# A chunked scan: Gram products with the two heads alternating on the array's row halves, and chunk decays read from the running sums by ScalarE

## The chip, the cores and the metric

The kernel runs as one program on one core of one Trainium2 chip. The metric is the device time of one execution in microseconds (us). The engines named below are TensorE (PE, with its weight loads listed as PEld), VectorE (DVE), ScalarE (ACT), GpSimdE (POOL) and the DMA queues that SyncE (SP) issues. They run side by side and wait for each other through semaphores.

## What is computed

Two transformer blocks follow each other on 256 tokens of width 2048, all in float32. The first is a differential attention with a short convolution and a gated feed-forward. The second puts 16 meta tokens ahead (272 tokens in all), and has two branches: a gated linear recurrence (RWKV-7) with 16 heads of 64, and an attention with forget gates. The change lies in the recurrence:

```
def step(S, inp):                       # per head, S is 64 x 64
    r_t, w_t, k_t, v_t, a_t, b_t = inp
    sa = einsum('bhvk,bhk->bhv', S, a_t)
    S  = S * w_t[:, :, None, :] + sa[..., None] * b_t[:, :, None, :] + v_t[..., None] * k_t[:, :, None, :]
    return S, einsum('bhvk,bhk->bhv', S, r_t)
```

`w_t` is a decay per channel. The kernel does not step through 272 tokens. It cuts them into three chunks (16, 128 and 128 tokens) and works with products of whole chunks.

## The kernel before, in words

**The big products.** Nearly all of the time goes into dense layers whose weights come from memory in units of 1 MB (`w_raw`). ACT rounds a unit to `w_hi`, DVE subtracts to get `w_lo`, and PE makes three products (`hi*hi`, `lo*hi`, `hi*lo`) for each tile of 128 x 128 weights.

**The recurrence** runs in eight steps `j`, each for two heads, which lie on partitions 0 to 63 and 64 to 127 of one tile. `rwkv_pe`, `rwkv_act` and `rwkv_dve` hold the instruction streams of a step, written out by hand. The order on an engine is the order of the code. One counting semaphore per engine (`rp`, `ra`, `rd`) carries the names of the steps: `did(("gram", j))` adds one, and `after(("gram", j))` waits for it.

Between the pieces of a step stands `side(n)`. It puts in `n` slots of a dense layer that runs beside the recurrence (lines L468, L470, L472 on PE: six matmuls a slot; L450 on ACT and L455 on DVE prepare its weights). So while PE waits in the recurrence it has other work, as much as is put there. The side work goes on after the recurrence; a slot that isn't used is not lost.

The places in one step that matter here, in order on PE:

- **sums** (L1627 to L1629): for each chunk, the log decays `ld` (stationary) times a table of ones and zeros. L1627 gives the inclusive running sums in PSUM bank 4, L1628 the exclusive ones in bank 3. Both are counted from the chunk's middle: `mid` is 1 for the first half of the chunk, and is subtracted. L1629 gives three more columns for each chunk in bank 5: the sum over the first half, over the second half, and over all.
- ACT then takes exponentials (L1854 to L1857). The last one, over 9 columns, is `eaux`: the decays from a chunk's start to its middle, from the middle to its end, and over all of it.
- DVE builds the scaled tensors `bh`, `kh` and `ar` from them (L1971 to L1975), PE transposes some (**toks**, L1641 and L1645).
- **gram** (L1659, L1661, L1664): the products of `bh` and `kh` with `ar` within each chunk, for each head. A product contracts over the 64 channels of one head, so its operands lie on one half of the partitions. Of each 128 x 128 result, L1659 makes the upper 64 rows and L1661 the lower right quarter (the other quarter is above the diagonal and masked). L1664 makes the 16 x 16 results of the meta tokens. Head `h`, source `n` and chunk `c` go to PSUM bank `2 * n + h`. The 16 x 16 results of both heads lie in bank 4.
- After `gram`, PE does four slots of side work. DVE masks the results and starts to invert a triangular matrix with PE and ACT in turns (L1989, L2026 to L2061; L1675 on PE).
- Later in the step the recurrent `state` is carried from chunk to chunk (L2082 to L2103) with the columns of `eaux`.

One float32 matmul of the code shows as two MATMUL records in the trace, each with its weight load. An f32 product in the dense layers (`fp32r`) shows as one.

Of the kernel before, what the change touches and what calls it, by code (L numbers as in the profile page):

```python
# [48 lines left out]
def constants():  # L49

    p = np.arange(P)
    parts = {}
    parts["ident"] = np.eye(P)
    half = (p[:, None] // RHD) == (p[None, :] // RHD)
    parts["head_sum"] = half.astype(float)
    parts["head_center"] = np.eye(P) - half / RHD
    s, t = p[:, None], p[None, :]
    parts["gram_mask"] = np.concatenate([s < t, s <= t], axis=1)
    parts["upper8"] = (s < t) & (s // 8 == t // 8)
    parts["lower8"] = (s > t) & (s // 8 == t // 8)  # L60
    for m in (16, 32, 64, 128):
        parts[f"join{m}"] = (s // m == t // m) & (s % m < m // 2) & (t % m >= m // 2)

    def sums(n):
        s, t = np.arange(n)[:, None], np.arange(n)[None, :]
        mid = (s <= n // 2 - 1).astype(float)
        incl, excl = (s <= t) - mid, (s < t) - mid
        aux = np.concatenate([mid, 1 - mid, np.ones((n, 1))], axis=1)
        m = np.concatenate([incl, excl, aux], axis=1) * DECAY_SCALE
        return np.concatenate([m, np.zeros((P - n, m.shape[1]))], axis=0)  # L70

    parts["sums"] = sums(P)
    parts["sums_meta"] = sums(META)
    k = np.arange(TOK)[None, :]
    parts["fox_mask"] = np.where(k <= P + META + p[:, None], 0.0, MASKED)
    sel = np.zeros((P, 46))
    sel[:64, 14], sel[64:, 15] = 1, 1
    parts["half_to_row"] = sel
    sel = np.zeros((P, 15))
    sel[:, 7] = 1  # L80
    parts["tile_to_row"] = sel
    parts["causal_tokens"] = s <= t

    dist = 255 - np.arange(SEQ + P - 1)
    n = np.maximum(dist, 0)
    exact = BUCKETS // 2
    nf = np.maximum(n, exact).astype(np.float32)
    large = exact + (np.log(nf / np.float32(exact)) / np.float32(math.log(MAX_DIST / exact))
                     * np.float32(BUCKETS - exact)).astype(np.int32)
    bucket = np.where(n < exact, n, np.minimum(large, BUCKETS - 1))  # L90
    hot = np.zeros((P, dist.size))
    hot[bucket, np.arange(dist.size)] = 1
    parts["bucket_hot"] = hot
    parts["line_mask"] = np.tile(np.where(dist >= 0, 0.0, MASKED), (P, 1))
    at, out = {}, []
    n = 0
    for name, a in parts.items():
        at[name] = (n, n + a.shape[1])
        out.append(a.astype(np.float32))
        n += a.shape[1]  # L100
    return np.concatenate(out, axis=1), at
# [33 lines left out]
def transformer_pair_kernel(nc, a, out, table_at):  # L135

    ctx = ExitStack()
    with ctx:
# [1291 lines left out]
        def place(*shape):  # L1430
            nonlocal at0
            v = area(at0, *shape)
            at0 += int(np.prod(shape))
            return v
# [20 lines left out]

        xs, us = (diff[:, 1, n * P:(n + 1) * P].rearrange("p (h v) -> p h v", h=2) for n in range(2))
        ys = shift[:, 0:SEQ]
        eaux = place(9)
        assert at0 <= ARENA, at0
        y_sq = gm.rearrange("p q (a t) -> p (q a) t", a=2)  # L1460
        rows_kk = small2[0:LANES, 0]
# [124 lines left out]
        def rwkv_pe(side):  # L1586
# [33 lines left out]
            for j in range(8):  # L1620
                side(3)
                pe.wait_ge(*rd.after(("ld", j)))
                for n, t in enumerate(PIECES):
                    rows = t.stop - t.start
                    tb = T["sums_meta" if n == 0 else "sums"]
                    lhs = ld[0:rows, n, :]
                    pe.matmul(psum[:, 4, t], lhs, tb[0:rows, 0:rows], start=True, stop=True)  # L1627
                    pe.matmul(psum[:, 3, t], lhs, tb[0:rows, rows:2 * rows], start=True, stop=True)  # L1628
                    mm = pe.matmul(psum[:, 5, 3 * n:3 * n + 3], lhs, tb[0:rows, 2 * rows:2 * rows + 3],  # L1629
                                   start=True, stop=True)  # L1630
                mm.then_inc(*rp.did(("sums", j)))
                side(2)
                pe.wait_ge(*rd.after(("rk", j)))
# [15 lines left out]

                pe.wait_ge(*rd.after(("bv", j)))  # L1650
                pe.wait_ge(*ra.after(("toks", j)))
                for h in range(2):
                    r = slice(h * RHD, (h + 1) * RHD)
                    for c in range(2):
                        t0 = META + c * P
                        for n, src in enumerate((bh, kh)):
                            o = psum[:, 2 * n + h, 2 * P * c:2 * P * (c + 1)].rearrange(
                                "p (a t) -> p a t", a=2)
                            pe.matmul(o[0:64], src[r, t0:t0 + 64], ar[r, :, t0:t0 + P],  # L1659
                                      start=True, stop=True)  # L1660
                            pe.matmul(o[64:P, :, 64:P], src[r, t0 + 64:t0 + P],  # L1661
                                      ar[r, :, t0 + 64:t0 + P], start=True, stop=True)
                    for n, src in enumerate((bh, kh)):
                        mm = pe.matmul(psum[mh[h], 4, n * META:(n + 1) * META], src[r, 0:META],  # L1664
                                       ar[r, 0, 0:META], start=True, stop=True)
                mm.then_inc(*rp.did(("gram", j)))
# [145 lines left out]
        def rwkv_act(side):  # L1812
# [30 lines left out]
            for j in range(8):  # L1843
# [10 lines left out]
                s.activation(ar[:, 0], psum[:, 3, 0:TOK], ACT.Exp)  # L1854
                s.activation(ar[:, 1], psum[:, 4, 0:TOK], ACT.Exp)
                s.activation(einv, psum[:, 4, 0:TOK], ACT.Exp, scale=-1.0)
                s.activation(eaux, psum[:, 5, 0:9], ACT.Exp).then_inc(*ra.did(("exp", j)))  # L1857
                side(4)
                s.wait_ge(*PEA("toks"))
                s.activation(toks.rearrange("p a b -> p (a b)"), psum[:, 1, :], ACT.Copy)  # L1860
# [51 lines left out]
        def rwkv_dve(side):  # L1912
# [32 lines left out]
            for j in range(8):  # L1945
# [120 lines left out]
                for h in heads:  # L2066
# [12 lines left out]
                    .then_inc(*D_("u0"))  # L2079
                side(1)  # L2080
                v.wait_ge(*PEA("s0"))
                v.tensor_scalar(state, psum[:, 2, 0:RHD], eaux[:, 1:2], None, ALU.mult) \  # L2082
                    .then_inc(*D_("s0"))
                v.wait_ge(*A_("s0"))
                v.tensor_scalar(state_h, state, eaux[:, 3:4], None, ALU.mult).then_inc(*D_("sh1"))
                side(2)
                for c in (1, 2):
                    v.wait_ge(*PEA(f"x{c}"))
                    v.tensor_copy(xs, psum[:, 0:2, 0:RHD]).then_inc(*D_(f"x{c}"))
                    side(1)  # L2090
                    v.wait_ge(*PEA(f"u{c}"))
                    v.tensor_copy(us, psum[:, 3, 0:P].rearrange("p (h v) -> p h v", h=2)) \
                        .then_inc(*D_(f"u{c}"))
                    side(1)
                    if c == 1:
                        v.tensor_scalar(state, state, eaux[:, 5:6], None, ALU.mult).then_inc(*D_("sd"))
                        v.wait_ge(*PEA("y1s1"))
                        v.wait_ge(*A_("sd"))
                        v.scalar_tensor_tensor(out=state, in0=psum[:, 2, 0:RHD], scalar=eaux[:, 4:5],
                                               in1=state, op0=ALU.mult, op1=ALU.add) \  # L2100
                            .then_inc(*D_("s1"))
                        v.wait_ge(*A_("s1"))
                        v.tensor_scalar(state_h, state, eaux[:, 6:7], None, ALU.mult) \  # L2103
                            .then_inc(*D_("sh2"))
                        side(2)
                v.wait_ge(*PEA("y2"))
# [658 lines left out]
```

## Time and profile before

| | |
|---|---|
| median of three runs | 3148.33 us (3145.39 to 3151.86) |
| the profiled execution | 3146.21 us, its span 3144.3 us |
| mean granted clock of TensorE | 0.977 |
| PE busy | 3001.1 us, 95% of the span |
| DVE busy | 1737.0 us, 55% |
| ACT busy | 1238.6 us, 39% |
| L1659, L1661, L1664, L1629 on PE | 128, 128, 64 and 48 records |

A record is one instruction as the profiler saw it. Records of PE overlap, as their ends are modelled; the distance from one start to the next says more of what one costs than its length does. The recurrence lies between about 1500 and 1990 us of the span.

### The profile page before, as it was taken

How to read it: one execution, taken by the hardware profiler on the slowest of the kernel's cores; microseconds unless marked ns; L12 is line 12 of the kernel's file. 1: busy time of each engine (PE TensorE's matmuls, PEld its weight loads, DVE VectorE, ACT ScalarE, POOL GpSimd, SP SyncE). 2: the span in 40 equal slices, each digit the busy share in tenths (PEclk: the TensorE clock that was granted, in tenths of full speed). 3: DMA queues.
4: the chain of work that ended last, by engine and by line, in shares of the span. 5: the costliest groups of instructions: out<-in, count | busy, mean ns of one | idle time of the engine just before them, and what ended most of it. 6: DMA issues, size and time to landing. Idle time of an engine off the chain costs nothing.

```text
span 3144.3 us, 57107 instructions
## 1 busy us (share of the span) xinstructions
PE 3001.1 (95%) x24369; PEld 2880.7 (92%) x24369; DVE 1737.0 (55%) x2618; ACT 1238.6 (39%) x1799; POOL 68.8 (2%) x108
## 2 busy tenths in 40 slices
PE   7999889999999998997999999998999999999999
PEld 6999889999999998997778888796999999999999
DVE  5467556455555446545656566575656454555444
ACT  4345345333334334434323232355334333333343
POOL 1001000000000000000000000000000000000000
PEclk9999899999999998999999999998999999999999
DMA  5665344555555554454222322542554555555553
GB/s 198 205 173 158 114 161 161 185 183 181 185 187 187 186 182 140 160 168 129 79 70 70 83 78 55 147 131 72 188 175 161 187 186 183 182 184 186 187 187 135
DMA packets 370309, 484.89 MB, mean 154 GB/s; under 512 B 12359, under 2 KB 181654, under 8 KB 370150
## 3 DMA queue, kind: packets, MB, share of 16 engines
q1 hardware_dynamic: 362752, 471.55, 47.2%
q0 software_dynamic: 4112, 7.88, 0.9%
q10 hardware_dynamic: 3302, 3.39, 0.3%
q8 instruction: 109, 1.79, 0.2%
q14 instruction: 34, 0.28, 0.0%
HBM read 475.76 MB, written 7.01 MB: 154 GB/s over the span
## 4 chain that ended last, share of the span: by engine, by line
PE 87%; DVE 8%; ACT 3%; issue 1%; DMA 0%; SPq 0%; DVEq 0%; ACTq 0%
PE psum L339 21%; PE psum L337 21%; PE psum L338 21%; PE psum L468 5%; PE psum L472 4%; PE psum L470 4%; PE psum L1675 3%; DVE w_lo L319 1%; PE psum L1659 1%; DVE w_lo L455 1%; ACT w_hi L310 1%; DVE arena L1989 1%; DVE arena L773 0%; PE psum L2391 0%; DVE arena L1992 0%
## 5 line engine op out<-in xcount | busy, mean ns | idle before, releaser
L337 PE MATMUL psum<-act_hi,w_hi 128*128 128x256 f32 (+1 forms) x5840 | 1651.9, 283 | 64.9 <-DVE act_lo L864 18.1
L338 PE MATMUL psum<-act_lo,w_hi 128*128 128x256 f32 (+1 forms) x5840 | 1655.0, 283 | 0.0
L339 PE MATMUL psum<-act_hi,w_lo 128*128 128x256 f32 (+1 forms) x5840 | 1654.1, 283 | 0.0
L319 DVE TENSOR_TENSOR w_lo<-w_raw,w_hi 128x1024 fp32r<-128x1024 f32 x728 | 858.7, 1221 | 894.0 <-ACT w_hi L310 893.9
L310 ACT ACTIVATE w_hi<-w_raw 128x1024 fp32r<-128x1024 f32 x728 | 730.6, 1051 | 1204.7 <-PE psum L339 1204.7
L337 PEld LDWEIGHTS psum<-act_hi,w_hi 128*128 128x128 f32 x5840 | 1111.2, 190 | 72.0 <-issue 32.4
L339 PEld LDWEIGHTS psum<-act_hi,w_lo 128*128 128x128 f32 x5840 | 1112.4, 190 | 0.0
L338 PEld LDWEIGHTS psum<-act_lo,w_hi 128*128 128x128 f32 x5840 | 1104.5, 189 | 0.3
L468 PE MATMUL psum<-act_hi,w_hi 128*128 128x256 f32 (+1 forms) x1280 | 393.5, 307 | 0.9 <-DVE arena L1352 0.9
L472 PE MATMUL psum<-act_hi,w_lo 128*128 128x256 f32 (+1 forms) x1280 | 366.3, 286 | 0.0
L470 PE MATMUL psum<-act_lo,w_hi 128*128 128x256 f32 (+1 forms) x1280 | 366.3, 286 | 0.0
L450 ACT ACTIVATE w_hi<-w_raw 128x512 fp32r<-128x512 f32 x320 | 195.9, 628 | 292.7 <-PE psum L472 278.1
L455 DVE TENSOR_TENSOR w_lo<-w_raw,w_hi 128x512 fp32r<-128x512 f32 x320 | 219.5, 704 | 92.9 <-ACT w_hi L450 92.3
L468 PEld LDWEIGHTS psum<-act_hi,w_hi 128*128 128x128 f32 x1280 | 245.9, 192 | 24.3 <-issue 14.8
L470 PEld LDWEIGHTS psum<-act_lo,w_hi 128*128 128x128 f32 x1280 | 246.2, 192 | 1.0
L472 PEld LDWEIGHTS psum<-act_hi,w_lo 128*128 128x128 f32 x1280 | 246.0, 192 | 0.0
L1675 PE MATMUL psum<-arena 128*128 128x128 f32 (+1 forms) x800 | 125.8, 304 | 23.8 <-DVE arena L2035 17.0
L1675 PEld LDWEIGHTS psum<-arena 128*128 128x128 f32 (+1 forms) x800 | 107.7, 204 | 39.6 <-DVE arena L2035 18.1
L620 DVE TENSOR_TENSOR arena<-psum,rstd 128x256 f32<-128x256 f32 (+1 forms) x200 | 79.3, 420 | 54.8 <-PE psum L339 48.9
L1871 ACT ACTIVATE arena<-psum 128x256 f32<-128x256 f32 x96 | 36.9, 385 | 111.1 <-PE psum L1675 111.1
L1989 DVE TENSOR_TENSOR arena<-psum,tab 64x512 f32<-64x512 f32 (+1 forms) x24 | 20.6, 858 | 31.9 <-PE psum L1664 31.7
L2055 DVE TENSOR_TENSOR arena<-psum,arena 128x256 f32<-128x256 f32 (+1 forms) x56 | 21.3, 393 | 19.7 <-PE psum L1675 17.6
(383 smaller groups left out, 1566.8 us busy)
## 6 DMA issues: line engine op xcount, KB each, us to landing
w_raw<-w_in SPq DMA_DIRECT2D x128, 1024.0 KB, 5.7
w_raw<-w_down SPq DMA_DIRECT2D x88, 1024.0 KB, 5.1
w_raw<-w_gate_up SPq DMA_DIRECT2D x88, 1024.0 KB, 5.0
w_raw<-w_gate SPq DMA_DIRECT2D x44, 1024.0 KB, 5.1
w_raw<-w_up SPq DMA_DIRECT2D x44, 1024.0 KB, 5.1
w_raw<-w_out SPq DMA_DIRECT2D x16, 1024.0 KB, 5.1
w_raw<-w_o SPq DMA_DIRECT2D x16, 1024.0 KB, 5.1
w_raw<-w_branch_a SPq DMA_DIRECT2D x8, 1024.0 KB, 5.0
```

Source lines behind the costliest of these rows:

```text
L310: nc.scalar.activation(w_hi[:, s % 2, 2 * h:2 * h + 2, 0:wd], w_raw[:, s % RAW, 2 * h:2 * h + 2, 0:wd], ACT.Copy).then_inc(hi_ready, 1)
L319: nc.vector.tensor_tensor(w_lo[:, s % 2, 2 * h:2 * h + 2, 0:wd], w_raw[:, s % RAW, 2 * h:2 * h + 2, 0:wd], w_hi[:, s % 2, 2 * h:2 * h + 2, ...
L337: pe.matmul(dst, w1, x1, start=first, stop=False, skip_group_check=True)
L338: pe.matmul(dst, w1, x0, start=False, stop=False, skip_group_check=True)
L339: mm = pe.matmul(dst, w0, x1, start=False, stop=stop and k == UNIT_K - 1, skip_group_check=True)
L450: nc.scalar.activation(side_view(w_hi, u % 2, 4 * n, 4), side_view(w_raw, u % RAW, 4 * n, 4), ACT.Copy).then_inc(hi_ready if n % 2 else si ...
L455: nc.vector.tensor_tensor(side_view(w_lo, u % 2, 4 * n, 4), side_view(w_raw, u % RAW, 4 * n, 4), side_view(w_hi, u % 2, 4 * n, 4).bitcast( ...
L468: pe.matmul(dst, hi[:, k], act_hi[:, k, tok], start=k == 0, stop=False, skip_group_check=True)
L470: pe.matmul(dst, hi[:, k], act_lo[:, k, tok], start=False, stop=False, skip_group_check=True)
L472: mm = pe.matmul(dst, lo[:, k], act_hi[:, k, tok], start=False, stop=k == KT - 1, skip_group_check=True)
L620: nc.vector.tensor_tensor(dst(m), psum[:, m, 0:SEQ], rstd[:, X], ALU.mult) \
L1675: return of_head(h, meta, lambda q, m: pe.matmul(ps(bank, q, m), sl(l, q, m), sl(r_, q, m), start=True, stop=True))
```

## The change

Three edits in the recurrence, and nothing elsewhere.

1. **Gram order.** The outer loop over the heads goes. For each chunk and source, the matmul of head 0 is followed by that of head 1, first for the upper 64 rows, then for the lower quarter. All 16 x 16 products come at the end, with the heads alternating as well. The same matmuls write to the same places.
2. **No third product.** The three columns per chunk (L1629) are no longer computed: 24 matmuls, 48 records in all. ACT reads two columns of each of the running sums: the exclusive sum at a chunk's first token is minus its first half, and the inclusive sum at the last token of a chunk is its second half. So one activation of 9 columns becomes two of 2 columns (`to_mid`, `from_mid`), both from PSUM with a stride.
3. **State.** Where the state was multiplied by the decay over the whole chunk (`eaux[:, 5:6]`), the already scaled `state_h` is multiplied by `from_mid`. That adds a wait for `sh1`, which DVE itself has finished before.

```
-        aux = np.concatenate([mid, 1 - mid, np.ones((n, 1))], axis=1)
-        m = np.concatenate([incl, excl, aux], axis=1) * DECAY_SCALE
+        m = np.concatenate([incl, excl], axis=1) * DECAY_SCALE
...
-                    pe.matmul(psum[:, 3, t], lhs, tb[0:rows, rows:2 * rows], start=True, stop=True)
-                    mm = pe.matmul(psum[:, 5, 3 * n:3 * n + 3], lhs, tb[0:rows, 2 * rows:2 * rows + 3],
-                                   start=True, stop=True)
+                    mm = pe.matmul(psum[:, 3, t], lhs, tb[0:rows, rows:2 * rows], start=True, stop=True)
...
-                for h in range(2):
-                    r = slice(h * RHD, (h + 1) * RHD)
-                    for c in range(2):
-                        t0 = META + c * P
-                        for n, src in enumerate((bh, kh)):
-                            o = psum[:, 2 * n + h, 2 * P * c:2 * P * (c + 1)].rearrange(
-                                "p (a t) -> p a t", a=2)
-                            pe.matmul(o[0:64], src[r, t0:t0 + 64], ar[r, :, t0:t0 + P],
+                for c in range(2):
+                    t0, t1 = META + c * P, META + c * P + 64
+                    for n, src in enumerate((bh, kh)):
+                        o = [psum[:, 2 * n + h, 2 * P * c:2 * P * (c + 1)].rearrange("p (a t) -> p a t", a=2)
+                             for h in range(2)]
+                        for h, r in enumerate(hs):
+                            pe.matmul(o[h][0:64], src[r, t0:t1], ar[r, :, t0:t0 + P], start=True, stop=True)
+                        for h, r in enumerate(hs):
+                            pe.matmul(o[h][64:P, :, 64:P], src[r, t1:t1 + 64], ar[r, :, t1:t1 + 64],
                                       start=True, stop=True)
-                            pe.matmul(o[64:P, :, 64:P], src[r, t0 + 64:t0 + P],
-                                      ar[r, :, t0 + 64:t0 + P], start=True, stop=True)
-                    for n, src in enumerate((bh, kh)):
+                for n, src in enumerate((bh, kh)):
+                    for h, r in enumerate(hs):
                         mm = pe.matmul(psum[mh[h], 4, n * META:(n + 1) * META], src[r, 0:META],
                                        ar[r, 0, 0:META], start=True, stop=True)
...
-                s.activation(eaux, psum[:, 5, 0:9], ACT.Exp).then_inc(*ra.did(("exp", j)))
+                s.activation(to_mid, psum[:, 3, META:META + P + 1:P], ACT.Exp, scale=-1.0)
+                s.activation(from_mid, psum[:, 4, META - 1:META + P:P], ACT.Exp) \
+                    .then_inc(*ra.did(("exp", j)))
...
-                        v.tensor_scalar(state, state, eaux[:, 5:6], None, ALU.mult).then_inc(*D_("sd"))
+                        v.wait_ge(*A_("sh1"))
+                        v.tensor_scalar(state, state_h, from_mid[:, 1:2], None, ALU.mult).then_inc(*D_("sd"))
```

On TensorE, the Gram products of a step before: the end of head 0 and the start of head 1 (64x256 is the upper part, 64x2x64 the lower quarter, 16x16 the meta tokens).

```order
L1659 MATMUL psum<-arena 64x256
L1661 MATMUL psum<-arena 64x2x64
L1659 MATMUL psum<-arena 64x256
L1661 MATMUL psum<-arena 64x2x64
L1664 MATMUL psum<-arena 16x16 x2
L1659 MATMUL psum<-arena 64x256
L1661 MATMUL psum<-arena 64x2x64
```

The same place now, up to the side work behind it (the lines are one or two lower in the changed file).

```order
L1657 MATMUL psum<-arena 64x256 x2
L1659 MATMUL psum<-arena 64x2x64 x2
L1657 MATMUL psum<-arena 64x256 x2
L1659 MATMUL psum<-arena 64x2x64 x2
L1663 MATMUL psum<-arena 16x16 x4
L467 MATMUL psum<-act_hi,w_hi 128x272
```

Each x2 is head 0, then head 1. The 16x16 products stood behind each head, and now stand once behind both.

On ScalarE, the exponentials of a step and what stands behind them, before:

```order
L1854 ACTIVATE arena<-psum 128x272
L1855 ACTIVATE arena<-psum 128x272
L1856 ACTIVATE arena<-psum 128x272
L1857 ACTIVATE arena<-psum 128x9
L450 ACTIVATE w_hi<-w_raw 128x512
L1860 ACTIVATE arena<-psum 128x512
```

And now:

```order
L1853 ACTIVATE arena<-psum 128x272
L1854 ACTIVATE arena<-psum 128x272
L1855 ACTIVATE arena<-psum 128x272
L1858 ACTIVATE arena<-psum 128x2
L1859 ACTIVATE arena<-psum 128x2
L449 ACTIVATE w_hi<-w_raw 128x512
```

One instruction more stands ahead of the rounding of the next side weights.

## Rows read from the trace of the kernel before

**Rows 1.** The page: PE's busy time, and the chain by engine

```profile
PE 3001.1 (95%) x24369; PEld 2880.7 (92%) x24369; DVE 1737.0 (55%) x2618; ACT 1238.6 (39%) x1799; POOL 68.8 (2%) x108
...
PE 87%; DVE 8%; ACT 3%; issue 1%; DMA 0%; SPq 0%; DVEq 0%; ACTq 0%
```

**Rows 2.** Windows, Gram to Gram: us, busy PE, PEld, DVE, ACT, POOL; PEclk, DMA

```profile
1759.28:1819.91 60.63, 57.08 (x461) 49.08 (x460) 37.51 (x98) 17.59 (x44) 2.62 (x5) 0.97 0.27 73
1819.91:1878.57 58.66, 55.05 (x461) 47.55 (x461) 37.47 (x97) 21.85 (x49) 0.00 (x0) 1.00 0.28 72
```

**Rows 3.** Timeline of PE, step 1's Gram products: start, length, [idle before]

```profile
1572.45 0.43 PE L1659 MATMUL psum<-arena 64*64 64x256 f32 x1
1572.46 0.43 PE L1661 MATMUL psum<-arena 64*64 64x128 f32 x2
1572.72 0.38 PE L1659 MATMUL psum<-arena 64*64 64x256 f32 x1
1572.93 0.38 PE L1659 MATMUL psum<-arena 64*64 64x256 f32 x1
...
1574.32 0.26 PE L1664 MATMUL psum<-arena 64*16 64x16 f32 x4
1574.51 0.43 PE L1659 MATMUL psum<-arena 64*64 64x256 f32 x1
...
1576.38 0.26 PE L1664 MATMUL psum<-arena 64*16 64x16 f32 x4
1576.57 0.39 PE L468 MATMUL psum<-act_hi,w_hi 128*128 128x272 f32 x1
```

**Rows 4.** Timeline and line view, L1145: row halves alternate in block one's attention

```profile
184.46 0.93 PE L1145 MATMUL psum<-arena 64*128 64x128 f32 x8
185.31 0.39 PE L468 MATMUL psum<-act_hi,w_hi 128*128 128x256 f32 x1
...
L1145 PE MATMUL psum<-arena x8: 272/374/378, 184.5 to 185.0; 64*128 64x128 f32 x4, 64*128 64x256 f32 x4
```

**Rows 5.** Timeline of PE, running sums of step 1

```profile
1564.37 0.36 PE L1629 MATMUL psum<-tab,arena 16*128 16x3 f32 x2
1564.65 0.49 PE L1627 MATMUL psum<-tab,arena 128*128 128x128 f32 x2
...
1565.34 0.47 PE L1627 MATMUL psum<-tab,arena 128*128 128x128 f32 x2
1565.65 0.39 PE L1628 MATMUL psum<-tab,arena 128*128 128x128 f32 x2
1565.87 0.28 PE L1629 MATMUL psum<-tab,arena 128*128 128x3 f32 x2
1566.01 0.37 PE L468 MATMUL psum<-act_hi,w_hi 128*128 128x272 f32 x1
```

**Rows 6.** Timeline of step 1: from the exponentials to the transposes

```profile
1567.04 0.20 ACT L1857 ACTIVATE arena<-psum 128x9 f32<-128x9 f32 x1
1567.10 1.34 ACT L450 ACTIVATE w_hi<-w_raw 128x512 fp32r<-128x512 f32 x2
...
1567.78 0.69 DVE L455 TENSOR_TENSOR w_lo<-w_raw,w_hi 128x512 fp32r<-128x512 f32 x1 [1.83 <-ACT w_hi L450]
...
1569.22 0.43 DVE L1972 TENSOR_TENSOR arena<-arena 128x272 f32<-128x272 f32 x1
...
1569.71 0.65 PE L1641 MATMUL psum<-tab,arena 128*128 128x128 f32 x4
1570.30 0.51 PE L1645 MATMUL psum<-tab,arena 64*16 64x64 f32 x12
1570.74 0.39 PE L468 MATMUL psum<-act_hi,w_hi 128*128 128x272 f32 x1
```

**Rows 7.** Timeline behind Gram: DVE (step 5), then PE (step 1)

```profile
1824.14 1.22 DVE L1989 TENSOR_TENSOR arena<-psum,tab 64x1024 f32<-64x1024 f32 x1 [3.19 <-PE psum L1664]
...
1584.13 3.53 PE L1675 MATMUL psum<-arena 128*128 128x128 f32 x15 [2.37 <-DVE arena L2035]
```

More of the change, by code:

```diff
@@ L1457, in transformer_pair_kernel @@
         ys = shift[:, 0:SEQ]
-        eaux = place(9)
+        to_mid, from_mid = place(2), place(2)
         assert at0 <= ARENA, at0
@@ L2081, in rwkv_dve @@
                 v.wait_ge(*PEA("s0"))
-                v.tensor_scalar(state, psum[:, 2, 0:RHD], eaux[:, 1:2], None, ALU.mult) \
+                v.tensor_scalar(state, psum[:, 2, 0:RHD], from_mid[:, 0:1], None, ALU.mult) \
                     .then_inc(*D_("s0"))
                 v.wait_ge(*A_("s0"))
-                v.tensor_scalar(state_h, state, eaux[:, 3:4], None, ALU.mult).then_inc(*D_("sh1"))
+                v.tensor_scalar(state_h, state, to_mid[:, 0:1], None, ALU.mult).then_inc(*D_("sh1"))
                 side(2)
@@ L2095, in rwkv_dve @@
                     if c == 1:
-                        v.tensor_scalar(state, state, eaux[:, 5:6], None, ALU.mult).then_inc(*D_("sd"))
+                        v.wait_ge(*A_("sh1"))
+                        v.tensor_scalar(state, state_h, from_mid[:, 1:2], None, ALU.mult).then_inc(*D_("sd"))
                         v.wait_ge(*PEA("y1s1"))
                         v.wait_ge(*A_("sd"))
-                        v.scalar_tensor_tensor(out=state, in0=psum[:, 2, 0:RHD], scalar=eaux[:, 4:5],
+                        v.scalar_tensor_tensor(out=state, in0=psum[:, 2, 0:RHD], scalar=from_mid[:, 1:2],
                                                in1=state, op0=ALU.mult, op1=ALU.add) \
@@ L2102, in rwkv_dve @@
                         v.wait_ge(*A_("s1"))
-                        v.tensor_scalar(state_h, state, eaux[:, 6:7], None, ALU.mult) \
+                        v.tensor_scalar(state_h, state, to_mid[:, 1:2], None, ALU.mult) \
                             .then_inc(*D_("sh2"))
```

## The prediction, made before the changed kernel ran

> **What bounds the kernel now.** I read the page first. TensorE is busy for 95% of the span, and the chain that ended last runs through it for 87% [rows 1]: a microsecond less on TensorE is a microsecond less in the time, unless another engine is late in the same place. Then the windows, cut from one step's Gram products to the next's. There are eight steps of about 61 us, and TensorE is busy for 57 of 60.6 us in one of them, VectorE for 37.5 and ScalarE for 17.6 [rows 2]. The reader is to see two things there. No other engine is near its limit over a step. And the step with a granted clock of 1.00 took 58.66 us while the one ahead of it, at 0.97, took 60.63: a stretch at 1.2 GHz costs a step about 2 us. It is the only one of the eight at 1.00.
>
> Last the timeline of TensorE, which gives the price of each part. Behind Gram, VectorE is what TensorE waits for: it stands idle until the last 16x16 product is there (3.19 us in the step shown), starts masking at once, and TensorE later waits 2.37 us for it [rows 7]. So the end of Gram releases both engines, and all that follows in the step moves with it.
>
> **The Gram products.** In step 1 the first record of L1659 starts at 1572.45, the 16x16 products of head 0 at 1574.32, head 1 at 1574.51, and the side work at 1576.57 [rows 3]. So one head takes 2.06 us and both 4.12. Within a head the records of L1659 follow each other every 0.21 to 0.22 us (1572.72, 1572.93), eight of them. Those of L1661 start within 0.01 us of them and add nothing: they use the other half of the array's columns. The rest, some 0.35 us a head, is the first weight load, the gap of about 0.3 us from the last start of L1659 to L1664, and the 0.19 us from there to the next shape. So a head is a queue of eight records on one square of the array, and the other head's square, with other rows, is empty all that time.
>
> Do two row halves work at the same time when they share their columns? L1145 is such a place in this kernel: halves alternate, each writes its own bank. Its eight records, four over 128 columns and four over 256, would take 4 x 0.11 + 4 x 0.215 = 1.3 us one after the other at the rate of L1659. The next shape starts after 0.85 us, switch included [rows 4]. At full overlap they need 0.65 us plus 0.2 for the switch, which is 0.85. So the halves overlap fully there.
>
> The new order puts head 1's record right behind head 0's. Four squares then have work, and the longest queue is still eight records of L1659. I expect first start to side work to take what one head takes now, 2.06 us, so 4.12 - 2.06 = 2.06 us less in a step. The 16x16 products are a point apart. Four records more now stand in the one place, head by head. At the worst they run behind the first four, which costs as much as those do, 0.19 us; so 1.87 to 2.06 us are saved. Over eight steps that is 15.0 to 16.5 us. I take 16.2, near the upper end, since they cost little each.
>
> The Trainium skill, TensorEngine Tiling (Array Packing), Restrictions and Gotchas, says that different row tiles can't access one PSUM bank at the same time. That speaks against these 16x16 products alone, since both heads write bank 4; by it the lower end, 15.0, would hold. The transposes of L1645 alternate the heads into one bank as well, and their twelve records take 0.44 us with the switch [rows 6], 0.04 each, so the trace shows no long turns.
>
> Is something late next? VectorE finishes what stands ahead of its masks 3.19 us before they may start in the step shown [rows 7]. Of that 2.06 goes, so 1.1 us of cover stay and nothing is given back. If that cover were gone, the part beyond it would be lost. The amount of side work behind Gram stays four slots, and VectorE's chain behind Gram is as long as it was, so the wait of 2.37 us stays.
>
> **The third product of the sums.** L1629 has two records for each of three chunks, on the way between `ld` and the side work. In the second and third chunk they cost what lies between their start and the next: 1565.87 to 1566.01 is 0.14 us [rows 5]. In the first it is 0.28, which includes a change of shape that stays; I count 0.2. And the records of L1627 after such a short product take 0.31 us (1565.34 to 1565.65) where those of L1628 take 0.22: the load of the next weights isn't covered by so short a matmul. That is 0.09 more. The sum is 0.2 + 0.14 + 0.14 + 0.09 = 0.57; with the short loads not won back it is 0.48, with all of the 0.28 it is 0.65. I take 0.55, so 4.4 us over eight steps, with ends at 3.8 and 5.2. It is on the path: what follows on ScalarE, VectorE and TensorE waits for the last of these sums and moves forward with it.
>
> **ScalarE's extra activation.** The one over 9 columns is followed by the next after 0.06 us, though it is 0.20 long [rows 6]. Two over 2 columns cost one start more: 0.06 us, and 0.20 if they didn't overlap. Behind it stands the rounding of side weights, for which VectorE waits 1.83 us; its `kh` then ends at 1569.65, and the transposes start at 1569.71. So in a step like this the 0.06 us reaches TensorE. I count 0.4 us over eight steps, and nothing or 1.6 us at the ends.
>
> **The rest.** VectorE's new wait is for its own result of several instructions before, and TensorE's `u1` and VectorE's copy lie between: nothing; if it cost anything it would be hidden ahead of `y1s1`, which TensorE delivers later. The table loaded at the start is six columns narrower: nothing.
>
> **The sum.** -16.2 - 4.4 + 0.4 = -20.2 us. Against the profiled execution, 3146.21 us, that is 3126.0. The median of the runs is 2.1 us above it, which gives 3128.1. I take 3127.
>
> The clock is added to neither. The stretches at 1.2 GHz come behind Gram in the gap where TensorE waits. Steps that are 2.6 us shorter will meet them at other moments. Three more or three fewer over the scan, at 2 us each, is 6 us either way, and I have no reason for one sign.
>
> **Rivals.**
>
> *Records start strictly in program order (10%).* Then for each chunk and source head 1's first record can't start ahead of head 0's second. With 0.22 and 0.11 us as steps: 0, 0.22 for head 0, 0.22, 0.44 for head 1, then 0.44, 0.55 and 0.55, 0.66 for the quarters. Four such groups take 2.65 us, and with 0.3 and 0.19 behind them Gram takes 3.1 instead of 4.12 us. That saves 1.0 us a step, 8 in all, and with the sums 12: 3135 us. Against it: L1661's first record starts 0.01 us after L1659's first, while L1659's second, which is ahead of it in the program, starts only at 1572.72 [rows 3].
>
> The Trainium skill states this rule (TensorE: Matmul & The Clock Gate, Part 3, The mechanism): matmuls start and end in strict order of the program, without reordering. By that rule, 3135 us; the trace disagrees with it for the starts, so it gets a small chance.
>
> *Row halves with the same columns take turns (4%).* L1145 [rows 4] speaks against it. Then sixteen records of L1659 at 0.215 us and one switch less leave 4.0 us of 4.12. With the sums that makes 5 to 6 us: 3142.
>
> *More time at the lower clock (3%).* The Gram products are half as long, and TensorE's thin stretch follows sooner. If each step caught one stretch more than now, at 2 us each [rows 2], 16 us of the 20 were lost: 3143.
>
> *All four squares take turns (3%), the one that ends slower.* No row shows four squares at work at once, only two. If alternating made every record wait for the one before, Gram would take 16 x 0.215 + 16 x 0.108 = 5.2 us and 0.5 around it, 5.7 against 4.12. That is 1.6 us more in each of eight steps, 12.6 in all, less 4 from the sums: 3156. It decides from a Gram of 4.6 us on. Against it speak the two column halves of L1659 and L1661, which overlap at full rate, and the two row halves of L1145.
>
> **How the numbers follow.** The forecast has 80%. Its own ends are -15.0 - 3.8 + 1.6 = -17.2 (3130) and -16.5 - 5.2 = -21.7 (3125), and the clock adds 6 on either side: about 3119 to 3136. For the range I take 3118 to 3137, which takes in the first rival. About 0.2%, 6 us, is what a measurement of this kernel can tell from no change. Forecast, first rival and half of the second lie beyond it: faster 0.93, the same 0.04, slower 0.03.
>
> **What would show it.** In the changed profile the 64x256 records start in pairs, 0.01 us apart, every 0.21 to 0.22 us, and from the first of them to the side work it is 2.1 to 2.2 us. VectorE's idle time ahead of its first mask falls by 2 us in each step. The sums of a step take 0.5 to 0.6 us less. TensorE's waits at L1641 grow by 0.1 us at most. The prediction is wrong if pairs start 0.2 us apart, if Gram takes more than 2.5 us, or if TensorE's waits behind Gram grow by what Gram has lost.

## The result and the profile after

The changed kernel took 3124.76 us (median of four runs, 3124.32 to 3130.45) beside 3150.1 us (3145.39 to 3152.05). The ratio is 0.9926, with a 95% interval of 0.9909 to 0.9943. Measured again with other runs of the kernel before, it took 3124.18 us beside 3145.06 us: a ratio of 0.9935 (0.9920 to 0.9950). So the change is worth 21 to 25 us, and 3127 had been predicted. The changed kernel gave nearly the same time both times. It is the time of before that differed by 5 us between the comparisons. The 3150.1 us is the median of only four of its runs, the 3145.06 us that of nine. Over all 37 runs of the kernel before that are on record the median is 3146.4 us, some 22 us above the changed kernel's.

The profiled execution took 3125.17 us, its span is 3123.2 us. On the page of the profile, the answers to [rows 1]:

```profile
PE 2976.8 (95%) x24321; PEld 2862.3 (92%) x24321; DVE 1737.4 (56%) x2618; ACT 1239.0 (40%) x1807; POOL 68.9 (2%) x108
...
PE 87%; DVE 9%; ACT 3%; issue 1%; DMA 0%; SPq 0%; DVEq 0%; ACTq 0%
```

The 48 records that went are L1629's, and ACT has eight more. VectorE's busy time didn't change. TensorE's share of the chain is the same: it is as much the bound as before.

The timeline of TensorE through one step's Gram products (start, length; the upper products are L1657 now, the quarters L1659, the 16x16 ones L1663), the answer to [rows 3]:

```profile
1574.19 0.43 PE L1657 MATMUL psum<-arena 64*64 64x256 f32 x2
1574.20 0.43 PE L1659 MATMUL psum<-arena 64*64 64x128 f32 x4
1574.45 0.38 PE L1657 MATMUL psum<-arena 64*64 64x256 f32 x2
1574.47 0.39 PE L1659 MATMUL psum<-arena 64*64 64x128 f32 x4
...
1575.32 0.81 PE L1657 MATMUL psum<-arena 64*64 64x256 f32 x6
1576.06 0.27 PE L1663 MATMUL psum<-arena 64*16 64x16 f32 x8
```

The side work behind it starts at 1576.26, 2.07 us after the first record, where it was 4.12. The x2 and x4 are to be read with the lengths: two records of L1657, each 0.43 us long, fit into 0.43 us, so they start together. The next pair comes after 0.26 and then every 0.22 us, as the single ones did. The eight 16x16 records need 0.27 us, where four needed 0.26. In all eight steps Gram takes 2.07 us.

The sums and ScalarE's exponentials in the same step, the answers to [rows 5] and [rows 6]:

```profile
1566.15 0.39 PE L1626 MATMUL psum<-tab,arena 16*128 16x16 f32 x2
1566.39 0.37 PE L1627 MATMUL psum<-tab,arena 16*128 16x16 f32 x2
1566.69 0.49 PE L1626 MATMUL psum<-tab,arena 128*128 128x128 f32 x2
1567.02 0.39 PE L1627 MATMUL psum<-tab,arena 128*128 128x128 f32 x2
1567.24 0.39 PE L1626 MATMUL psum<-tab,arena 128*128 128x128 f32 x2
1567.46 0.39 PE L1627 MATMUL psum<-tab,arena 128*128 128x128 f32 x2
1567.60 0.37 PE L467 MATMUL psum<-act_hi,w_hi 128*128 128x272 f32 x1
...
1568.73 0.19 ACT L1858 ACTIVATE arena<-psum 128x2 f32<-128x2 f32 x1
1568.79 0.20 ACT L1859 ACTIVATE arena<-psum 128x2 f32<-128x2 f32 x1
1568.84 1.20 ACT L449 ACTIVATE w_hi<-w_raw 128x512 fp32r<-128x512 f32 x2
```

From the first record of the sums to the side work it is 1.46 us (1566.15 to 1567.60); it was 2.12. The third chunk's L1626 is followed after 0.22 us and no longer after 0.31. The two short activations start 0.06 us apart, each about 0.2 us long.

Behind Gram, the answers to [rows 7], and from the list of waits of TensorE in the scan (total, times, longest) two lines of the changed kernel, then one of before:

```profile
1808.71 1.22 DVE L1992 TENSOR_TENSOR arena<-psum,tab 64x1024 f32<-64x1024 f32 x1 [1.18 <-PE psum L1663]
...
1583.83 4.46 PE L1674 MATMUL psum<-arena 128*128 128x128 f32 x21 [2.37 <-DVE arena L2038]
...
PE psum L1674 <- DVE arena L2038: 17.0, 8, 2.5
PE psum L1674 <- DVE arena L2031: 4.6, 8, 0.7
...
PE psum L1675 <- DVE arena L2035: 17.0, 8, 2.5
```

VectorE's idle time ahead of its masks fell from 3.19 to 1.18 us, by what Gram lost, and TensorE's wait behind it is 2.37 us as before, 17.0 us over the scan in both kernels. The gain was not given back there. The smaller waits behind grew by 1.1 us over the scan: from 4.4 to 4.6 us for L2031 (L2028 before), and from 1.9 to 2.8 us for L2048 (L2045 before).

### The profile page after: what moved, and what is told of

Its sections match the earlier page's. It is cut to its first block, busy times and chain, and to the rows that moved or that the text cites. A ratio compares the mean times of both kernels' runs of the same rounds, so it can differ in the third digit from the quotient of the medians.

```text
span 3123.2 us, 57019 instructions
## 1 busy us (share of the span) xinstructions
PE 2976.8 (95%) x24321; PEld 2862.3 (92%) x24321; DVE 1737.4 (56%) x2618; ACT 1239.0 (40%) x1807; POOL 68.9 (2%) x108
## 4 chain that ended last, share of the span: by engine, by line
PE 87%; DVE 9%; ACT 3%; issue 1%; DMA 0%; SPq 0%; DVEq 0%; ACTq 0%
PE psum L338 21%; PE psum L337 21%; PE psum L336 21%; PE psum L467 5%; PE psum L471 4%; PE psum L469 4%; PE psum L1674 3%; DVE w_lo L318 1%; DVE w_lo L454 1%; DVE arena L1992 1%; ACT w_hi L309 1%; DVE arena L772 0%; PE psum L2395 0%; DVE arena L1995 0%; PE psum L1657 0%
## 5 line engine op out<-in xcount | busy, mean ns | idle before, releaser
L1674 PEld LDWEIGHTS psum<-arena 128*128 128x128 f32 (+1 forms) x800 | 105.7, 201 | 40.5 <-DVE arena L2038 18.1
L717 ACT ACTIVATE act_hi<-res,vec 128x256 fp32r<-128x256 f32 (+1 forms) x64 | 27.2, 499 | 11.0 <-DVE res L841 8.7
```

The lines of the kernel that those rows point to most:

```text
L1674: return of_head(h, meta, lambda q, m: pe.matmul(ps(bank, q, m), sl(l, q, m), sl(r_, q, m), start=True, stop=True))
```

## The experiments

Unless it is said otherwise, an experiment's kernel is the changed one with the edit shown, in short form, and a step's Gram time is from its first 64x256 record to the side work (or the next shape) behind it.

### Each half of the change alone

`gram_only` is the kernel before with the new Gram order. `sums_only` is the changed kernel with the old one:

```
 # gram_only: kernel before, plus
-for h in range(2):  for c in range(2):  for n, src in ...:  upper(h); quarter(h)   # then 16x16 of h
+for c in range(2):  for n, src in ...:  upper(0); upper(1); quarter(0); quarter(1)
+for n, src in ...:  16x16 of head 0; of head 1
 # sums_only: changed kernel, with the - order in place of the + order
```

> The kernel before with the new Gram order alone; the third product of the sums and its exponentials stay. Theory (the two heads' squares of the array work at once): from the first 64x256 record of a step to the side work 2.07 us instead of 4.12, so 8 x 2.05 = 16.4 us less than before, some 3132 us; the sums keep their 2.12 us a step. Rival (most of the 25 us between the medians comes from the clock or from the sums, and the wait behind Gram takes part of it back): less than 10 us below before, and TensorE's wait of 2.4 us behind Gram grows.

> The changed kernel with the old Gram order (head by head). Theory: the sums of a step take 1.54 instead of 2.12 us, the extra activation costs 0.06 us, so 8 x 0.52 = 4.2 us less than before, some 3144 to 3146 us; Gram takes 4.12 us. Rival (the sums lie beside other work, or the two activations cost as much as they save): within 1 us of before, with TensorE's wait at the transposes of the odd steps longer by 0.5 us.

`gram_only` took 3131.84 us, `sums_only` 3142.58 us, and the kernel before 3146.28 us beside them (ratios 0.9961, interval 0.9949 to 0.9974, and 0.9985, interval 0.9974 to 0.9997). So the Gram order alone is worth 14.4 us and the sums with their exponentials 3.7; each theory's difference came within 2 us, though `sums_only` is 1.4 us below the 3144 to 3146 us that were expected. The runs of `sums_only` spread from 3135 to 3148 us, and the interval of its gain reaches from 1 to 8 us. The two gains add up to 18.1, below the 20.9 of both together, by less than the intervals allow.

The profiles are sharper. Gram takes 2.07 us in `gram_only` and 4.12 in `sums_only`. And one step ran at full clock in both, so that its length can be compared. First `sums_only`, then `gram_only`, windows from the first step's Gram to the second's (length, then busy PE, PEld, DVE, ACT, POOL, granted clock, DMA share, GB/s):

```profile
1510.97:1570.44 59.47, 55.96 (x456) 48.17 (x455) 36.37 (x95) 17.72 (x45) 3.84 (x7) 1.00 0.30 83
```

```profile
1514.19:1572.13 57.94, 54.55 (x462) 47.55 (x461) 36.37 (x95) 17.75 (x44) 3.84 (x7) 1.00 0.31 85
```

The difference is 1.53 us: 2.05 of Gram, less 0.52 that the sums are worth in such a step. The sums alone can be read at one clock as well. The step of before that ran at 1.00 took 58.66 us [rows 2], and the same step of `sums_only`:

```profile
1814.67:1872.62 57.95, 54.31 (x455) 46.80 (x455) 37.46 (x97) 21.88 (x50) 0.00 (x0) 1.00 0.28 74
```

That is 0.71 us less. TensorE's wait of 17.0 us behind Gram is the same in both halves, and so the two rival views fall by these rows: neither gain is taken back behind its place. By the times alone they would not, since the intervals reach down to 8 us for the one and 1 us for the other.

### Would the hardware find the overlap in any order?

```
 # head_major
+for h in range(2):  for c in range(2):  for n, src in ...:  upper(h); quarter(h)
+for n, src in ...:  16x16 of head 0; of head 1
```

> The changed kernel, with the Gram products head by head again and only the 16x16 products of both heads together at the end. Tells whether the hardware would find the overlap by itself in any order. Theory (it looks only a few matmuls ahead): head 1 starts when head 0 is nearly done; Gram takes 16 x 0.216 + 0.5 = 3.9 to 4.0 us a step. Rival (every square has a long queue of its own, so the order hardly matters): 2.1 to 2.5 us.

The timeline of TensorE in the second step of `head_major` (L1658 upper, L1660 quarters, L1664 16x16):

```profile
1568.33 0.43 PE L1658 MATMUL psum<-arena 64*64 64x256 f32 x1
...
1568.81 0.38 PE L1658 MATMUL psum<-arena 64*64 64x256 f32 x1
...
1569.03 0.59 PE L1658 MATMUL psum<-arena 64*64 64x256 f32 x2
...
1569.26 0.43 PE L1658 MATMUL psum<-arena 64*64 64x256 f32 x1
1569.26 0.43 PE L1660 MATMUL psum<-arena 64*64 64x128 f32 x3
...
1571.12 0.27 PE L1664 MATMUL psum<-arena 64*16 64x16 f32 x8
1571.32 0.39 PE L467 MATMUL psum<-act_hi,w_hi 128*128 128x272 f32 x1
```

Gram takes 2.99 us, so both theories missed. The row of 1569.03 with x2 is head 0's fourth record and its fifth, 0.22 us later. At that moment, 0.92 us after the start, head 1's first begins (1569.26), though head 0 still has three 64x256 records that have not started. From there the heads run together. The overlap begins early by itself, but not at once, and it costs 0.92 us a step against alternating. The single run of 3128.55 us is 4.4 us above the changed kernel; 8 x 0.92 would be 7.4, and one run cannot tell these apart. The third step can, which ran at full clock in both. First `head_major`, then the changed kernel:

```profile
1629.08:1687.89 58.81, 54.83 (x455) 47.62 (x454) 36.81 (x96) 17.77 (x45) 3.73 (x7) 1.00 0.29 79
1633.37:1691.27 57.90, 53.91 (x456) 46.87 (x455) 36.83 (x96) 17.77 (x45) 3.73 (x7) 1.00 0.30 80
```

The step is 0.91 us longer, so what Gram loses there reaches the whole step.

### All upper products ahead of all quarters

```
 # quarters_last
+for c in range(2):  for n, src in ...:  upper(0); upper(1)
+for c in range(2):  for n, src in ...:  quarter(0); quarter(1)
```

> The changed kernel with all 64x256 products ahead of all 64x2x64 ones, heads alternating in both. Only two squares work at a time, one for each head. Theory (columns and rows overlap independently, and four squares cost nothing extra): the 64x256 records keep their distance of 0.216 us, and the quarters add nearly their own 8 x 0.108 us behind them, so Gram takes 2.7 to 3.0 us a step instead of 2.07. Rival A (four squares at once slow each other): the 64x256 records come closer than 0.216 us. Rival B (deep queues per square): the quarters still start early and Gram stays at 2.1 us.

```profile
1569.23 1.30 PE L1656 MATMUL psum<-arena 64*64 64x256 f32 x10
1570.16 0.44 PE L1662 MATMUL psum<-arena 64*64 64x128 f32 x4
1570.36 0.38 PE L1656 MATMUL psum<-arena 64*64 64x256 f32 x2
...
1571.18 0.27 PE L1666 MATMUL psum<-arena 64*16 64x16 f32 x8
1571.38 0.39 PE L467 MATMUL psum<-act_hi,w_hi 128*128 128x272 f32 x1
```

Gram takes 2.15 us (the one run took 3128.82 us, at a mean clock of 0.977 against 0.979 of the changed kernel). The quarters (L1662) start once five pairs of upper records have started, 0.93 us in, and then run beside the other three. So my theory missed again, and rival B was nearly right. Rival A is out: with two squares at work the upper pairs are 0.22 us apart, and with four as well (1570.36 and on).

Three kernels, the changed one, `head_major` and `quarters_last`, now agree on one picture. It is inferred from the starts; no row shows a queue. Records are handed out in the order of the program. A square of the array takes the one that runs and three more. When a square's queue is full, all that is behind waits. In `head_major` head 0's eighth record is handed out when its fifth starts, and head 1 follows at once. In `quarters_last` the same holds for both heads' eighth.

### A test of that picture

```
 # chunk_major
+for c in range(2):  for h in range(2):  for n, src in ...:  upper(h); quarter(h)
```

> The changed kernel with Gram by chunk, then head, then source: two 64x256 matmuls (four records) of head 0, then two of head 1. Head by head cost 0.92 us a step more than alternating, as head 1 started only when head 0's fifth record did. Theory (records are handed out in program order to a queue for each square, which holds the running one and three more; a full queue stops all behind it): four records fit, head 1 starts within 0.05 us of head 0, Gram takes 2.07 to 2.1 us. Rival (the look-ahead is a number of records in all, some 16 or fewer, or time based): head 1 starts 0.2 us or more behind head 0, and Gram takes 2.3 us or more.

```profile
1576.26 0.43 PE L1656 MATMUL psum<-arena 64*64 64x256 f32 x1
1576.27 0.32 PE L1657 MATMUL psum<-arena 64*64 64x128 f32 x1
1576.29 0.43 PE L1656 MATMUL psum<-arena 64*64 64x256 f32 x1
1576.30 0.43 PE L1657 MATMUL psum<-arena 64*64 64x128 f32 x3
```

Head 1's first record starts 0.03 us behind head 0's, with eight of head 0's ahead of it in the program, four of each kind. Gram takes 2.13 us, a little above the 2.07 to 2.1 expected, and far from the rival's 2.3. The single run took 3127.33 us.

That start alone doesn't rule out the rival. If TensorE looked at nine records in all, counted from the oldest that isn't done, the same starts would come out: the seventeenth record of `head_major` and of `quarters_last` begins when the ninth does, and here head 1's first record is the ninth. What rules it out is the next line of the timeline. Head 1's first quarter is the eleventh record, and it starts at 0.03 us as well (1576.30), while the very first record runs until 0.27 us. The same trace has head 0's quarters of the second chunk at 0.50 and 0.92 us, when its third and its fifth 64x256 record start, as the picture of a queue for each square wants it.

### Two row halves and one PSUM bank

```
-mm = pe.matmul(psum[mh[h], 4, n * META:(n + 1) * META], ...
+mm = pe.matmul(psum[mh[h], 4 + h, n * META:(n + 1) * META], ...     # and VectorE reads it there
```

> The changed kernel with the 16x16 products of head 1 in PSUM bank 5 instead of bank 4, where those of head 0 go; VectorE reads them there. Theory (one bank for two row halves costs nothing as long as the partitions differ): the eight records start as they do now, in pairs 0.01 us apart, four pairs in 0.09 us, Gram takes 2.07 us. Rival (the shared bank makes them take turns): the pairs come closer together and Gram gets shorter by up to 0.1 us.

The eight records take 0.27 us again, and Gram 2.07 (3124.05 us in one run). The shared bank costs nothing here, where the halves write different partitions of it (0 to 15 and 32 to 47).

### What Gram releases: a version that beats both

```
 # split_source
+for n, src in ...:  16x16 of head 0; of head 1
+for n, src in enumerate((bh, kh)):
+    for c in range(2):  upper(0); upper(1); quarter(0); quarter(1)
+    mm.then_inc(*rp.did(("gram" if n == 0 else "gramk", j)))
...
+v.wait_ge(*PEA("gramk"))
 gram_mask(1, [0])
```

> The changed kernel once more, on the chip of the three that follow. Theory: 8 x (2.05 + 0.58 - 0.06) = 20.6 us below before, give or take what the stretches at the lower clock differ by, so 3125 to 3128 against 3146 to 3150. Rival (the first comparison's 25 us were the change's full worth): 25 us below before again.

> The changed kernel with Gram in two parts: the 16x16 products first, then all products of bh, which release VectorE's first masks, then those of kh with a step of their own (gramk) that the second masks wait for. Nothing is added or left out. Theory (behind Gram VectorE's chain sets the pace, and TensorE waits 0.5 + 2.4 us for it in a step): VectorE's first mask starts 0.9 to 1.0 us earlier against Gram's start, and the start of TensorE's products behind the 2.4 us wait moves forward by as much; 8 x 0.9 = 7 us less than the changed kernel. Rival A (VectorE isn't ready sooner, its idle time of 1.15 to 1.3 us ahead of the masks is gone): no gain in the odd steps, under 4 us in all. Rival B (the wait returns later in the step): TensorE's waits at VectorE's L2038 shrink and those behind grow by the same, time within 1 us of the changed kernel.

`after_again` took 3124.18 us and `split_source` 3118.81, beside 3145.06 us before (`split_source`: ratio 0.9913, interval 0.9899 to 0.9926). So it is 5.4 us below the changed kernel, where 7 were expected. In its second step (VectorE, then the waits of TensorE in the scan):

```profile
1574.80 1.22 DVE L1992 TENSOR_TENSOR arena<-psum,tab 64x1024 f32<-64x1024 f32 x1 [0.44 <-PE psum L1663]
...
PE psum L1674 <- DVE arena L2039: 16.7, 8, 2.4
```

Gram starts at 1573.44 there, so the first mask comes 1.36 us behind it instead of 2.19: 0.83 us earlier. TensorE's wait of 4.6 us for L2031 is gone from the list, while the one for the p2t step is 16.7 us, 17.0 before. Both engines moved forward together. The third step ran at full clock in both kernels and is 0.83 us shorter (57.07 against 57.90 us). Rival A is out, as VectorE still had 0.44 us to spare; so is rival B.

`split_full_rows` adds one edit to it:

```
+v.memset(ld[:, 0], 0.0)                                     # once
-lhs = ld[0:rows, n, :]        # table rows tb[0:rows, ...]
+lhs = ld[:, n, :]             # table rows tb[:, ...]
```

> split_source, and the running sums of the 16 meta tokens contract over all 128 rows: the other rows of ld are zeroed once, and the table is zero there. The array keeps one shape through the sums. Theory: the change of shape between the first and second chunk costs 0.08 + 0.1 us, so the sums of a step take 1.35 instead of 1.54 us; 1.5 us less than split_source over eight steps, less than the runs can tell but visible in the profile. Rival (16 rows are loaded faster than 128): the sums take as long as before or longer.

The sums of a step take 1.26 us instead of 1.46, as expected. The time, 3117.43 us, is 1.4 below `split_source`, which the runs cannot tell from none.

The last one leaves TensorE as it is and moves two slots of VectorE's side work behind the p2t and ip2 steps (a transpose and an addition of the identity, by VectorE, in the inversion). TensorE has 30 products to do there:

```
 gram_mask(1, [0])
-side(2)
 for h in heads:  p2t; ip2
-side(2)
+side(4)
```

> split_full_rows, and VectorE's two slots of side work ahead of its p2t step move behind ip2, so that four slots stand there; TensorE's order is unchanged. Theory (VectorE's chain behind Gram sets the pace; TensorE waits 2.3 us a step for p2t, and the two slots ahead of it take 0.6 to 1.3 us, while the 30 products that follow on TensorE last longer than the four slots): TensorE's wait for p2t falls from 2.3 to 1.2 us in most steps, and the time by 4 to 8 us against split_full_rows (3117). Rival (the slots only change places: VectorE is late for ip4 by what it gained): TensorE waits as long later in the step, time within 1 us of split_full_rows or above it.

It took 3099.8 us beside 3147.9 (ratio 0.9847, interval 0.9833 to 0.9860), 17.6 us below `split_full_rows` and more than twice what was expected. The two were measured on different chips, each beside its own runs of before; the two profiled executions are 12.0 us apart (3115.09 and 3103.05). TensorE in one step of `split_late_side`, its waits in the scan, and three windows from Gram to Gram:

```profile
1579.19 2.76 PE L1674 MATMUL psum<-arena 128*128 128x128 f32 x20 [1.35 <-DVE arena L2039]
...
PE psum L1674 <- DVE arena L2039: 11.0, 8, 1.4
PE psum L1674 <- DVE arena L2049: 3.1, 8, 0.4
...
PE psum L1674 <- DVE arena L2043: 1.9, 4, 0.5
...
1571.52:1627.19 55.67, 53.00 (x461) 46.66 (x455) 37.54 (x97) 18.45 (x46) 3.72 (x7) 1.00 0.33 89
1627.19:1683.17 55.98, 53.15 (x461) 46.61 (x455) 36.73 (x96) 17.75 (x45) 3.72 (x7) 1.00 0.31 84
...
1848.30:1903.27 54.97, 52.12 (x461) 45.48 (x455) 37.09 (x97) 17.69 (x45) 0.00 (x0) 1.00 0.30 78
```

The same wait and windows in `split_full_rows`, and a stretch of its second step that lies right behind the wait:

```profile
1579.84 5.92 PE L1674 MATMUL psum<-arena 128*128 128x128 f32 x30 [2.31 <-DVE arena L2040]
...
PE psum L1674 <- DVE arena L2040: 16.7, 8, 2.4
...
1571.22:1629.09 57.87, 54.69 (x461) 48.11 (x455) 37.61 (x97) 18.46 (x45) 3.73 (x7) 0.97 0.32 85
1629.09:1687.40 58.31, 54.85 (x460) 48.05 (x454) 36.91 (x96) 17.75 (x45) 3.73 (x7) 0.97 0.29 80
...
1859.35:1914.90 55.55, 52.20 (x461) 45.47 (x455) 37.09 (x97) 17.70 (x45) 0.00 (x0) 1.00 0.29 77
...
1580.05:1583.46 3.41, 3.41 (x16) 3.07 (x16) 1.98 (x7) 0.38 (x1) 0.00 (x0) 0.50 0.97 264
```

The wait for p2t fell from 16.7 to 11.0 us over the scan. Of these 5.7 us some came back later in the step, as the rival said: 1.9 for L2043, which was no wait there before, and 0.7 more for L2049 (L2050 there, 2.4). A wait for a DMA (L1796) is 1.2 us longer as well. That leaves 1.9 us.

The rest goes with the clock. In the seven windows from the first Gram to the last, 401.5 us became 387.5. Of these 14.1 us TensorE's busy time makes 11.9, for the same products, and its idle time 2.1. In each of the first six windows of `split_full_rows` the clock was at 0.50, the lower of its two levels, for a while, in `split_late_side` in none. The last window ran at 1.00 in both kernels: there the busy time is the same (52.20 and 52.12), and the step is 0.6 us shorter by idle time alone. At that rate eight steps would gain 4.6 us, within the 4 to 8 of the theory, and the seven windows 4.1. So of the 14.1 us, 10 (the rest above 4.1) to 12 (all of the busy time) go with the clock. The theory had counted the wait and left the clock out. The medians lie 5.6 us further apart than the two profiled executions, and no row explains that part.

Why the clock no longer fell is less sure. In the first six steps of `split_full_rows` it fell 8.6 to 9.6 us behind the start of Gram, 0.2 to 1.4 us after the end of the wait for p2t (2.0 to 2.4 us long). In the last two steps the wait was 2.0 us too and the clock stayed. With waits of 1.36 to 1.42 us it stayed in all eight. So the wait in this thin stretch goes with the fall, but its length alone doesn't decide, and no run varies it by itself.

## Why the prediction was right

**Row halves overlap at full rate.** The Gram step had 4.12 us and was to have 2.06, and 2.07 was measured in every step: 8 x 2.05 = 16.4 us, where 16.2 were taken from a range of 15.0 to 16.5. The step that decided this was to look for another place in the same trace where halves alternate, L1145 [rows 4]. The two attached questions went the cheap way: the second 16x16 products cost 0.01 us and not 0.19, and VectorE had cover left.

**The sums.** 0.55 us a step were taken, and 0.66 was measured (2.12 to 1.46), just above the upper end of 0.48 to 0.65. The term that was too small is the third chunk: 0.14 counted, 0.22 measured, as the side work now follows 0.03 us after the last record of the sums, and came 0.11 after the last of L1629.

**ScalarE's activation** costs something in every other step. From the first record of the sums to the first of Gram the even steps are shorter by 0.66 to 0.67 us, so nothing is lost there. In the four odd steps, where ScalarE and VectorE are late for the transposes, it is 0.47 to 0.51: TensorE waits 0.12 to 0.13 us longer for them, a little more than the 0.1 that was given as the most. So some 0.17 us of the gain is lost in each of these four, 0.7 in all, where 0.4 was counted. Together that is 4 x 0.66 + 4 x 0.49 = 4.6 us, where 4.4 less 0.4 had been counted.

**The sum** of these parts is thus 16.4 + 4.6 = 21.0 us against 20.2 predicted, and the two profiled executions are 21.0 us apart (3146.21 and 3125.17). That this fits to a tenth is partly luck. The first Gram of the changed kernel starts 2.5 us later than that of before, though its sums are shorter, and the stretches from one Gram to the next get some 2 us shorter than the parts say, with less time at the lower clock. What lies outside the parts happened to add up to nothing.

**The spread of before.** The second comparison gives 20.9 us, the first 25.3. The 5 us between them lie in the runs of before, which range over 8 us in the second comparison, those of the changed kernel over 2. The mean granted clock of each run goes with it: of the 33 runs of before that were measured beside the experiments, the eleven at 0.979 or 0.980 took 3142.0 to 3144.1 us, and the twenty-two at 0.976 to 0.978 took 3144.8 to 3152.1 us. So 25 us is likely more than the change is worth.

**What a fall of the clock costs** was read too high. The 2 us came from a step at 0.97 (60.63 us) and the next one at 1.00 (58.66 us). In the changed kernel the same two steps both run at 0.97, and still take 58.18 and 57.36 us; so 0.8 us of the 2 is a difference between the steps. The windows of the last experiment give 1.6 to 1.7 us of busy time for one fall (54.69 against 53.00 us).

**The rivals.** Records in strict order of the program: out, as the quarters start at 1574.20 in the changed kernel, ahead of the second 64x256 records at 1574.45, and as `quarters_last` and `head_major` have later records start ahead of earlier ones too. Halves or all four squares in turns: out, by the pairs 0.01 us apart. More time at the lower clock: it did not come. Two steps of the changed kernel run at 1.00, where one did before; the prediction had no reason for either sign, so this was luck. The granted clock still mattered more than the prediction gave it, as the last experiment shows, only not for this change.

**The rules weighed.** That matmuls start in program order, which the Trainium skill states (TensorE: Matmul & The Clock Gate, Part 3, The mechanism), holds for the starts only within a square: across squares these traces show starts out of order, as long as no queue of a square is full. The ends of records are modelled and can't test the rest of it. That different row tiles cannot use one PSUM bank at once, as the Trainium skill says (TensorEngine Tiling (Array Packing), Restrictions and Gotchas), did not show as a cost in `meta_banks`, 0.27 us in both cases, with different partitions.

## What to carry to other kernels

Where small float32 products of several heads contract over half of the partitions, put those of different squares next to each other in the program: the order within the code is what starts them together. A run of eight records on one square gave 0.92 us of the overlap away, a run of four next to nothing. Look for another place in the same trace where the mechanism already works before pricing it. And look at what TensorE's clock does behind a wait: with a shorter one, some 4 us less for the wait came together with 10 to 12 us from a clock that no longer fell. Compare steps that ran at the same clock to keep the two apart.

## What the runs showed of the hardware

- The starts of four kernels fit a square of the array (64 rows by 64 columns) that takes four records, one running and three waiting, and a further record for it that holds up all behind, also those for idle squares: head 1 began 0.92 us late behind eight records of one square, and 0.03 us behind four.
- Four squares at once run as fast as one: 64x256 records every 0.22 us in each, with 64x128 ones beside them.
- Two row halves writing different partitions of one PSUM bank cost nothing: eight records in 0.27 us with one bank and with two.
- A matmul of three columns (two records) cost 0.14 us where it stood, and the matmul behind it 0.31 us instead of 0.22.
- Behind waits of TensorE of 2.0 to 2.4 us in a thin stretch the granted clock fell to 0.50 in six of eight steps; behind waits of 1.36 to 1.42 us in the same place it stayed at 1.00 in all eight. A fall cost 1.6 to 1.7 us of busy time in a step.
